# A fused decoder block on one core: on-chip copies of the first gate weights, an earlier first score block, split value blocks first, and mixer products in another order

## The reference

```python
h = rmsnorm(x); proj = h @ w_in                 # conv GLU | rwkv r,k,v | low rank | two gates
x = x + (g_conv * conv_branch + g_rw * rwkv7_branch) @ w_out
h = rmsnorm(x)
q = h @ w_q                                     # 8 heads x 2 halves x 128
s1, s2 = q . keys;  top 16 of each, top 16 of the 256 sums -> expert = e1*128 + e2
gate = softmax(best)
out[t] = sum_k gate[t,k] * gelu(u[e(t,k)] . h[t]) * v[e(t,k)]   # 16384 experts, 128 picks a token
y = rmsnorm(x + out)
```

## Time and profile before

| | |
|---|---|
| median of 3 runs | 1812.72 us (1811.16 to 1813.22) |
| the profiled execution | 1812.87 us, of which the span of instructions is 1810.9 us |
| mean granted clock of PE | 0.985 |
| PE, DVE, ACT, POOL busy | 96%, 78%, 41%, 33% of the span |
| moved by DMA | 399.06 MB, mean 220 GB/s |
| chain that ended last | PE 54%, issue 15%, POOL 4%, DMA 2% |

### The profile page before, as it was taken

The page is one execution under the profiler, slowest core; times in us unless marked ns, Lnnn a source line. Parts: engine busy times, 40 slices in busy tenths (PEclk is TensorE's granted clock), DMA queues, the critical chain, the costliest instruction groups (busy, mean ns, idle before and its releaser), DMA issues.

```text
span 1810.9 us, 33740 instructions
## 1 busy us (share of the span) xinstructions
PE 1745.3 (96%) x11997; PEld 1542.4 (85%) x11997; DVE 1421.2 (78%) x2759; ACT 737.1 (41%) x1049; POOL 593.5 (33%) x532
## 2 busy tenths in 40 slices
PE   5989999999979999999999899999999999999998
PEld 3878888877858799999999888888888888888887
DVE  5377777846479999979998588888888888888886
ACT  4464544352232233347777233333333333333333
POOL 0000000002000166678886344443333433334430
PEclk9999999989989999999999999999999999999999
DMA  4221121116222144456666999999999999999992
GB/s 162 82 71 37 49 77 55 54 66 243 94 75 77 69 160 159 159 175 251 223 223 228 352 377 367 367 361 349 336 330 343 343 348 348 347 361 339 336 335 84
DMA packets 157823, 399.06 MB, mean 220 GB/s; under 512 B 12432, under 2 KB 78096, under 8 KB 155696
## 3 DMA queue, kind: packets, MB, share of 16 engines
q1 hardware_dynamic: 118032, 252.20, 39.8%
q0 software_dynamic: 39712, 145.77, 21.5%
HBM read 353.88 MB, written 44.04 MB: 220 GB/s over the span
## 4 chain that ended last, share of the span: by engine, by line
PE 54%; issue 15%; POOL 4%; DMA 2%; DVE 1%; SPq 1%; ACT 0%; POOLq 0%; ACTq 0%; DVEq 0%
PE unit L382 54%; POOL uL L2105 4%; DMA vraw<-v_tab 1%; SPq L928 0%; DMA g_dram<-ge 0%; DMA sgw<-gate_dram 0%; DVE yo L2069 0%; SPq L941 0%; DVE accs L2006 0%; ACT vH L1011 0%; DVE aL L1981 0%; DVE mb L1836 0%; DVE uL L1945 0%; DVE wL L1471 0%; ACT sqj L1011 0%
## 5 line engine op out<-in xcount | busy, mean ns | idle before, releaser
L382 PE MATMUL unit<-h2H,uH 128*128 128x384 f32 x1024 | 355.8, 347 | 11.3 <-POOL uL L2105 9.1
L382 PE MATMUL unit<-h2H,uL 128*128 128x384 f32 x1024 | 344.9, 337 | 0.0
L382 PE MATMUL unit<-h2L,uH 128*128 128x384 f32 x1024 | 344.5, 336 | 0.0
L2133 POOL DMA_INDIRECT ring<-u_tab,idx x128 | 170.7, 1333 | 230.2 <-DVE accs L2006 198.1
L382 PE MATMUL unit<-vH,aH 128*128 128x512 f32 x768 | 238.6, 392 | 5.1 <-DVE vL L1987 5.1
L382 PE MATMUL unit<-vL,aH 128*128 128x512 f32 x768 | 237.7, 391 | 0.0
L382 PE MATMUL unit<-vH,aL 128*128 128x512 f32 x768 | 237.6, 391 | 0.0
L1987 DVE TENSOR_TENSOR vL<-vraw,vH 128x1024 fp32r<-128x1024 f32 x128 | 156.6, 1224 | 88.9 <-ACT vH L1011 88.5
L2133 POOL DMA_INDIRECT ring<-v_tab,idx x128 | 141.1, 1102 | 241.0 <-DVE ring L1992 238.3
L1011 ACT ACTIVATE aH<-af 128x384 fp32r<-128x384 f32 x128 | 67.0, 524 | 366.1 <-DVE af L1976 366.1
L382 PEld LDWEIGHTS unit<-h2H,uH 128*128 128x128 f32 x1024 | 193.9, 189 | 21.5 <-POOL uL L2105 16.1
(11 more groups left out here) (298 smaller groups left out, 3411.4 us busy)
## 6 DMA issues: line engine op xcount, KB each, us to landing
uraw<-uT SPq DMA_DIRECT2D x128, 512.0 KB, 7.6
vraw<-v_tab SPq DMA_DIRECT2D x128, 512.0 KB
wraw<-wall SPq DMA_DIRECT2D x68, 512.0 KB, 3.7
w_dram<-wst SPq DMA_DIRECT2D x12, 2048.0 KB, 6.7
wg<-w_dram SPq DMA_DIRECT2D x32, 768.0 KB
g_dram<-ge SPq DMA_DIRECT2D x64, 192.0 KB, 1.9
gl<-g_dram SPq DMA_DIRECT2D x32, 384.0 KB
gate_dram<-gst POOLq DMA_DIRECT2D x16, 256.0 KB, 2.4
```

Of the source, the lines that this page charges most:

```text
L382: return pe.matmul(out, lhsT, rhs, start=start, stop=stop, skip_group_check=True)
L2133: pool.indirect_dma_start(out=ring[k][:, :], out_offset=None, in_=(u_tab, v_tab)[half], in_offset=bass.IndirectOffsetOnAxis(ap=idx[:, SR * ...
```

## The change

- `inputs(t)`: the same 64 products, but the loop over the four kinds of product stands outside the loop over the four quadrants.
- PE does `whole(14)` ahead of products(1, 0) to (1, 2) instead of behind them.
- SP's first u loads wait for the last branch projection (`wo7`) instead of all splits; ACT splits block 0 (`uH`) after it has taken q14, once the last weight is split, instead of after the transposes.
- In the last round of W, SP fetches blocks 0 to 9 of group 0's weights, then gl, before the last store, and copies blocks 10 and 11 from wst on the chip; `load_wg(0, 0)` is gone. For this af moves to a place that wst does not cover, and DVE waits for four transfers instead of two.
- ACT does `v_high` before `a_high` for blocks 0 and 1 of a group.
- gfb moves in memory and is loaded when the last score is done.

```diff
--- before.py
+++ after.py
@@ -210,7 +210,7 @@
     aH = at("aH", 125, [P, G, TD], F32R)
     aL = at("aL", 131, [P, G, TD], F32R)
     gl = at("gl", 137, [P, 2, PRE, TD])
-    af = at("af", 143, [P, 2, TD])
+    af = at("af", 3, [P, 2, TD])
     wg = at("wg", 157, [P, 2, NTB, G, T_W])
     h2T = at("h2T", 187, [P, D])
     accs = at("accs", 177, [P, D])
@@ -222,7 +222,7 @@
     spa = at("spa", 186.375, [P, SR])
     ssq = at("ssq", 186.5, [P, TT])
     rsf = at("rsf", 186.5625, [P, TT])
-    gfb = at("gfb", 3, [P, D])
+    gfb = at("gfb", 36, [P, D])
     yo = at("yo", 12, [P, TT, D])
     sqj = at("sqj", 28, [P, D])
 
@@ -570,13 +570,15 @@
                 wait_taken(pe, f"keT{t}")
                 wait_taken(pe, f"rq{t}")
                 for i in range(CB):
-                    for p, q in ((0, 0), (1, 1), (0, 1), (1, 0)):
-                        hd = q * CB + i
-                        b_, y_ = u[half(q), p, i * HD:(i + 1) * HD], u[half(q), p, 256 + i * HD:256 + (i + 1) * HD]
-                        mm(b_, ke_tok[s][half(p), hd, :], v_tok[s][half(p), hd, :], i == 0, False)
-                        mm(y_, v_tok[s][half(p), hd, :], mrk[s][half(p), hd, :], False, False)
-                        mm(b_, bm[s][half(p), hd, 0:HD], ws[s][half(p), hd, HD:], False, False)
-                        last = mm(y_, ws[s][half(p), hd, HD:], bm[s][half(p), hd, HD:], False, i == CB - 1)
+                    for n in range(4):
+                        for p, q in ((0, 0), (1, 1), (0, 1), (1, 0)):
+                            hd = q * CB + i
+                            o = u[half(q), p, 256 * (n % 2) + i * HD:256 * (n % 2) + (i + 1) * HD]
+                            l, r = ((ke_tok[s][half(p), hd, :], v_tok[s][half(p), hd, :]),
+                                    (v_tok[s][half(p), hd, :], mrk[s][half(p), hd, :]),
+                                    (bm[s][half(p), hd, 0:HD], ws[s][half(p), hd, HD:]),
+                                    (ws[s][half(p), hd, HD:], bm[s][half(p), hd, HD:]))[n]
+                            last = mm(o, l, r, i == 0 and n == 0, i == CB - 1 and n == 3)
                 last.then_inc(fill_sem(f"B{t}"), 2)
 
             def state_of(c):
@@ -678,9 +680,9 @@
             norm_back(1)
             token_major(0)
             whole(13)
+            whole(14)
             for k in range(3):
                 products(1, k)
-            whole(14)
             token_major(1)
             masked_value(0, 1)
 
@@ -947,7 +949,7 @@
                 sp.dma_start(dst, ge[:, s, :]).then_inc(g_stored[s], 16)
 
 
-            sp.wait_ge(wl_ready, NW)
+            wait_filled(sp, f"wo{DC - 1}")
             for j in range(4):
                 load_u(pre_row(0, j), j)
             with sp.Fori(0, PRE_T // 4) as i:
@@ -958,7 +960,6 @@
             sp.wait_ge(ee_ready, 1)
             for g in range(G):
                 load_v(0, g)
-            sp.dma_start(gfb[:, :], gfrow).then_inc(gf_loaded, 16)
 
             def beside_w(i, last):
                 for j in range(4):
@@ -966,12 +967,25 @@
                     sp.wait_ge(ul_ready, n + 1)
 
                     load_u(G * (j // 2) + PRE + j % 2 if last else pre_row(PRE_T // 4 + i + 1, j), j)
+                    if last and j == 3:
+                        first_wg()
                     if j % 2:
                         sp.wait_ge(wst_ready, 2 + 16 * i + 8 * (j // 2) + 8)
                         b = j // 2
+                        if last:
+                            sp.dma_start(wg[:, 0, NTB - 2 + b], wst[:, b, 0:G, :]).then_inc(wg_loaded[0], 16)
                         sp.dma_start(w_dram[bass.ds(2 * i + b, 1)].rearrange("b p e t -> p (b e) t"),
                                      wst[:, b, :, :]).then_inc(wst_stored[b], 16)
                     store_g(n, j % 2)
+            def first_wg():
+                for i in range(2):
+                    sp.wait_ge(wst_stored[i], 16 * (NTB // 2 - 1))
+                sp.dma_start(wg[:, 0, 0:NTB - 2], w_dram[0:NTB - 2, :, 0:G, :].rearrange("b p e t -> p b e t")
+                             ).then_inc(wg_loaded[0], 16)
+                sp.wait_ge(wst_stored[0], 16 * NTB // 2)
+                sp.dma_start(gl[:, 0], g_dram[0:PRE].rearrange("n p t -> p n t")).then_inc(wg_loaded[0], 16)
 
             with sp.Fori(0, WI - 1) as i:
                 beside_w(i, False)
@@ -979,7 +993,6 @@
             for i in range(2):
                 sp.wait_ge(wst_stored[i], 16 * NTB // 2)
                 sp.wait_ge(g_stored[i], 16 * NPRE // 2)
-            load_wg(0, 0)
             load_wg(1, 1)
 
             def group_loads(q, par, more):
@@ -999,6 +1012,8 @@
                 group_loads(2 * i, 0, True)
                 group_loads(2 * i + 1, 1, True)
             group_loads(NG - 2, 0, False)
+            sp.wait_ge(scores_done, NK)
+            sp.dma_start(gfb[:, :], gfrow).then_inc(gf_loaded, 16)
             for n, t in enumerate((DT, *range(DT))):
                 sp.wait_ge(y_ready, n + 1)
                 sp.dma_start(y[t], yo[:, t, :]).then_inc(y_stored, 16)
@@ -1305,6 +1320,10 @@
                     wait_filled(act, f"sc{m - 2}")
                 fn(qt[:, m % 2, :], ps(f"q{m}")[:, :], ACT.Copy).then_inc(take_sem(f"q{m}"), 1)
                 split_h(W_Q + m + 2)
+                if m == 2 * PKH - 2:
+                    act.wait_ge(wl_ready, NW)
+                    act.wait_ge(u_loaded[0], 16)
+                    fn(uH[:, 0, :, :], uraw[:, 0, :, :], ACT.Copy).then_inc(uh_ready, 1)
             for name, dst in (("ht", h2T), ("xs", accs)):
                 for k in range(2):
                     wait_filled(act, f"{name}{k}")
@@ -1327,7 +1346,6 @@
                 u_high(n0 + 4 * i + j + 1, n0 // 4 + i + (j + 1) // 4, (j + 1) % 4)
 
             act.sem_inc(gelu_ready, 2)
-            u_high(0, 0, 0)
             for j in range(2):
                 ahead(0, 0, j)
                 gelu(j, j)
@@ -1413,8 +1431,8 @@
                 q = 2 * i + par
                 lap, base = NPRE // 4 + i + par, 2 * (1 - par)
                 for g in range(2):
+                    v_high(q, g)
                     a_high(q, g)
-                    v_high(q, g)
                 own_gelu(q, 0)
                 if more:
                     u_high(NPRE + 2 * (q + 1), lap, base)
@@ -1968,7 +1986,7 @@
 
                 q = 2 * i + par
                 if g == 0:
-                    dve.wait_ge(wg_loaded[par], 32 * i + 32)
+                    dve.wait_ge(wg_loaded[par], 32 * i + (32 if par else 64))
                 if g >= PRE:
                     dve.wait_ge(gelu_ready, NPRE + 2 * q + g - PRE + 3)
                 dve.wait_ge(al_ready, G * q + g + 1)
```

## The result

The changed kernel takes 1799.44 us (median of 4 runs, 1797.49 to 1800.68) beside 1811.94 us for the kernel before on the same chip: ratio 0.9939, 95% interval 0.9926 to 0.9952. Timed again with the experiments it gave 0.9942 (0.9928 to 0.9955). The forecast was 1795.4 us, 17.3 less than before, with a range of 1787 to 1804: the direction and the range hold, and 12.5 us of the 17.3 came.

A forecast was written before the change was run, and what follows sets the result against it. PE was taken as the bound, busy 1745.3 of 1810.9 us, so gains come from removing its stops or shortening its work; 5.4 + 0.5 + 1.7 + 5.2 + 4.5 = 17.3 us off 1812.72 gives 1795.4, range 1787 to 1804.

The forecast's parts named there:

- Part 1: Reordered inputs(t): 14.6 ns per instruction; 5.4 us kept for t = 0, 1 (first pair), 0.5 for t = 2, 3 (second).
- rival B: At inputs(t), sums into one place delay each other, half of 5.4 kept: 1798; or reorder fails: 1801.3 us; chance 0.15.
- Part 2: whole(14) ahead of products(1) fills a 4.58 us stop; VectorE's masks limit this to 3.4, less 1.7 low clock: 1.7 us.
- Part 3: First score block: PE waits only for ScalarE's last copy, 3.5 us earlier, plus 1.7 for the clock: 5.2 us.
- the shift survives the stage if the indices are there: Score stage: the 5.2 us gain lasts, since VectorE's last pick ends 8.4 us before PE's transposes.
- Part 4: First gated group: unit 0 5.1 us earlier, new 4.6 us stop at unit 1, later stop gone: 4.5 us gain.
- Rival A: First gated group: rows arrive in time, no stop at unit 1, 10.8 us instead of 4.5: 1789 us; chance 0.13.
- C: Stops only move: Part 2 and Part 4 give nothing, eaten by low clock and rows: 1801.6 us; chance 0.15.
- D: Gated groups slower: ScalarE's vH before aH lets late v blocks stop PE 1 us per group: 1826 us; chance 0.03.
- Edits at nothing: vH before aH in steady groups, late gfb load, and moving af and gfb in memory: claimed to cost or gain nothing.

The follow-up runs named there:

- rows_later: Changed kernel with VectorE's row work of even groups put behind the first two units' operands, rows 1 to 4 also behind the next uL: 1799.04 us, ratio 0.9938.
- operands_first: exp_later plus, in even groups, VectorE making the operands of units 0 to 2 and the next uL before any row: 1789.29 us, ratio 0.9888.
- exp_later: Changed kernel with ScalarE's wait for VectorE's picks and its Exp moved behind the next GELU and last u block's split: 1795.06 us, ratio 0.9915.

## Why the prediction was right or wrong

- **Part 1 (5.4 + 0.5).** Right in size: 4.6 us by the median, 4.8 to 5.5 by the two stretches above. The pace was as forecast (14.6 ns), and rival B, sums that hold each other up, is refuted. The shares came out otherwise, and that the total fits is in part luck. The first pair brought 3.1 instead of 5.4: 1.9 of the missing 2.3 us are PE standing still with no operand to wait for, until an instruction packet has come. The row that gave the pace held 32 instructions; the first pair has 320 in a row. The second pair brought 2.25 instead of 0.5. Its times came as worked out: inputs(3) waited 0.9 us for the bank, and chain(5) starts when VectorE's state is ready, 2.25 us earlier by this pair (forecast 2.3). But PE stood idle for 1.6 us before it, not some 3, and the clock stayed at 1.00 from 350 to 366 us, so the 1.7 us charged for it were not paid.
- **Part 2 (1.7).** Mechanism and size held within the noise: VectorE's masks are next, PE waits for them twice, 3.3 us, masked_value starts 3.3 us earlier (counted from the first low-rank product), and the clock falls after it (0.71 over 148 to 152 us), though not in every profile.
- **Part 3 (5.2).** The start came at full clock and 0.4 us earlier than forecast, and 5.9 us were gained there. The step that failed is "the shift survives the stage if the indices are there". It looked only at PE's transposes of the indices, with 8.4 us of slack behind the picks. ScalarE's Exp waits for the same picks, with a slack of 4.8 us, and has uH of the last block behind it. The picks were also taken to stay where they were; they came 2.6 us later, because two of VectorE's operations now start beside POOL's uL. 1.0 us was left.
- **Part 4 (4.5).** Unit 0 starts 5.3 us earlier after C (forecast 5.1); VectorE is held by row 0; 8.5 us from fetch to row is what the forecast had (1004.13 to 1012.6); the stop at unit 1 is 5.6 us (forecast 4.6), with the low clock after it (0.51 over 1010 to 1014); the stop one group later is gone. Measured 3.9 against 4.5. Rival A, rows in time, is refuted. The first packet of the fetch moved 4.4 to 4.7 us after the fetch began, before (1004.13) as after (996.31). The figure of about 1 us to the first byte in the Trainium skill, "DMA: Bandwidth & Descriptors", section "Latency and other measured facts", does not hold here.
- **Rivals C and D.** C named the kind of loss (two parts eaten by late engines) and put it on parts 2 and 4; it was part 3. D did not come: from 1100 to 1780 us PE has no idle time with vH ahead of aH.
- **Edits at nothing.** W to C is 185.99 us in both kernels, and the gated groups lost nothing. The late load of gfb was not tried by itself.

Taken together by stages (forecast and profile), 17.3 - 4.2 (part 3) - 0.6 (part 4) + 1.2 (S to Q) - 1.4 (start to S) = 12.3 us, the difference of the spans; the last two hold the noise told below.

## What to carry to other kernels

When a change lets the bound engine run ahead, list every wait of every engine on the work that does not move with it, and what is queued behind each; the least slack counts, not that of the bound engine's own wait. An engine's wait for late data belongs behind all that the bound engine needs from it, and a stop removed at one unit must be followed to the next operand in the same queue: rows_later gained nothing, operands_first 6.8 us over exp_later from C to the end (by the medians 0.0027, 4.9 us).

## What the runs showed of the hardware

- **The low clock comes and goes without a cause in the code.** Up to products(1) PE has the same instructions in all kernels, whole(14) aside, and near 70 us it is busy throughout, yet the clock granted near 70 us differs (kernel before, then the changed one):

```profile
68.00:72.00 4.00, 4.00 (x19) 0.63 0.41 133
72.00:76.00 4.00, 4.00 (x18) 0.95 0.01 2
```

```profile
68.00:72.00 4.00, 4.00 (x18) 0.55 0.43 131
72.00:76.00 4.00, 4.00 (x13) 0.60 0.01 4
```

  The first low-rank product starts between 75.0 and 78.5 us over the profiles, and only 0.8 us of that is there already at 38 us; 1.6 us of part 2's gain is lost in this way in the changed kernel's profile. A second such stretch, near 375 us, and a weight block that is ready near 414 us (PE idle 1.0 to 2.0 us) move S to Q between 353.5 and 358.2 us in kernels whose code there is the same or nearly so. A single profile is no measure of 2 us in these stages.
- **VectorE beside POOL.** `cand` (two inputs, 128x2048) took 3.87 to 3.90 us in all 11 cases over the 14 profiles in which it started during POOL's subtraction of a uL, and 2.29 in the 45 others. The shift of `c` (128x128) took up to 1.26 instead of 0.21; it was hit in the kernel before as well, in three of its four tiles. The extra time is what was left of POOL's operation. The reduction `ee` of the same size started during a uL 112 times and kept its 2.29 us, and the maxima and their index searches were not hit either. The product into `oneh` always starts during a uL and always takes 4.34 to 4.37 us; what it takes alone, no profile shows.
- **Short matmuls outrun their supply.** transfer(0) and inputs(0), 160 instructions at 28.8 and 14.6 ns, passed; in the next 160 PE stood still for 1.86 us, each time until 1.3 to 1.4 us after a packet of the instruction queue. In the second pair the wait of 0.9 us for the bank stands between, and only 0.2 to 0.75 us of such a stop is left behind inputs(3).
